# Attention values of a hybrid encoder block: three fp32r passes of split operands in place of fp32 products

## The chip, the cores and the metric

One core of a Trainium2 chip. The metric is the device time of one execution in microseconds (us). The core has five engines that run at the same time, each with a queue of its own: TensorE (PE, matrix products), VectorE (DVE), ScalarE (ACT), GpSimd (POOL) and SyncE (SP, which issues the loads here). They wait for each other by semaphores, and an engine that waits holds up everything behind the wait in its queue.

## What is computed

A block of a streaming encoder on 512 tokens of width 1024, all in fp32. Three branches (an S5 state space, a gated MLP with causal mixing, and a cross-attention into 256 memory tokens) are gated, summed, projected and added to x; a SwiGLU feed-forward with hidden width 2816 and a last RMS norm follow. What the change touches is the cross-attention, with 4 heads of width 128:

```python
kv = _rms(mem, g_mem) @ w_kv
k, v = jnp.split(kv, 2, axis=-1)
s = jnp.einsum('blhd,bmhd->bhlm', q, k) * (XA_HEAD_DIM ** -0.5)
p = jax.nn.softmax(s, axis=-1)
o = jnp.einsum('bhlm,bmhd->blhd', p, v)      # l: 512 tokens, m: 256 memory tokens
yc = o.reshape(bsz, seq, XA_WIDTH) @ w_c_out
```

## The kernel before, in words

**Split products.** Nearly all matrix products are made in three fp32r passes. An operand is kept as a high part, its value rounded to fp32r, and a low part, the value minus the high part, rounded too. `product(out, a, b, first, last)` issues high by high, high by low and low by high into one bank of PSUM (L1305 to L1307). The weights come as 512 KB tiles in a fixed order: SP loads tile t into one of two buffers (L314), ACT rounds it to `w_hi` (L460), POOL subtracts for `w_lo` (L383, or L388 in halves). Then TensorE uses the tile, and ACT may round the tile after next into the same slot. Small products stay in fp32: scores, transposes, the mixing of the gated MLP (L1477), and the products of probabilities and values (L1416).

**The attention stage**, 98 to 155 us in the trace. TensorE's order is written out by hand: `scores` of heads 0 and 1, then `value_weights(t)` (four tiles that build the values in banks 4 and 5) alternating with `zu(c)` (four tiles of the MLP's u half), with transposes and scores of later heads between them. It ends with

```python
value_weights(3)
zu(3)
pe.wait_ge(v_taken, 2)
values(0)
pe.wait_ge(exp_done, 16)
transposes(2)
values(1)
transposes(3)
```

then four mixing groups at L1477, `values(2)` and `values(3)`. The weight tiles of the gate stage (tile T_J1 and on) come next; the first gate matmul waits until DVE has added the mixing bias to all four groups (`sgu_taken`), because it uses their bank.

**One head.** `scores(h)` writes 512x256 scores. DVE finds the row maxima (`head_max`, L994 and L996), ACT takes the exponentials into `prob` (`softmax_exp`, L556), DVE multiplies by the reciprocal sums (`head_scale`, L1001 and L1004). `transposes(h)` turns `prob` into two banks, one for each half of the memory tokens (L1408, fp32). `take_pt(h)` exists twice: ACT copies the first half into `pT` (L568), DVE the second (L1011), at their own places in their queues. `values(h)` waits for both and issues one fp32 product for each half (L1416). `round_o(h)` on ACT and `low_o(h)` on DVE split the result for the output product.

**The values.** After `value_weights(3)` DVE scales banks 4 and 5 by the memory norm into `vM` (L1058), 128x512 for each of two token groups.

**The queues around it.** ACT, in order: ..., rounding of tile T_VU+7, gelu_u(2), rounding of T_J1, take_pt(1), softmax_exp(3), rounding of T_J1+1, gelu_u(3), take_pt(2), round_o(0), take_pt(3), round_o(1), four `round_yb`, round_o(2), round_o(3). DVE: ..., sine and cosine tables, scale_u(2), take_pt(1), head_max(3), `vM`, `table_sum`, scale_u(3), head_scale(3), take_pt(2), low_o(0), take_pt(3), low_o(1), the bias additions and gatings. POOL, after the low part of T_J1+1: memsets of `ca[1]` (L413) once `uc` is ready, of `st` after the transposes, of `ba` and `toep` after the mixing, then `pads_ready`, on which ACT's first `spread_b` waits, and the low parts of the further tiles.

Places in SBUF: `vM` lies right behind the keys `kT` (o_a + 12288 and o_a + 8192, 4 KB each); the buffer at o_u holds `uT` early and `ca[1]` later.

Of the kernel before, what the change touches and what calls it, by code (L numbers as in the profile page):

```python
# [16 lines left out]
P = 128  # L17
D = 1024
T = 512
M = 256  # L20
KD = D // P
WB = 512
# [3 lines left out]
HEADS = 4  # L26
# [50 lines left out]
def build(nc, xt_d, xtok_d, mem_d, mtok_d, small_d, sgu_d, w_d, out_d):  # L77
# [7 lines left out]
    with ExitStack() as ctx:  # L85
# [6 lines left out]
        def at(name, off, shape, dt=F):  # L92
            return nc.alloc_sbuf_tensor_at(name, shape, dt, offset=off)
# [33 lines left out]
        memf = at("memf", o_a, [P, KD, M])  # L127
        qT = at("qT", o_a, [P, HEADS, T])
        kT = at("kT", o_a + 8192, [P, HEADS, M])
        vM = at("vM", o_a + 12288, [P, 2, WB])  # L130
        mgf = at("mgf", o_a, [P, KD, T])

        vtok = at("vtok", o_b, [P, 4, WB])
# [41 lines left out]

        mstd = at("mstd", o_f, [P, M])
        mrstd = at("mrstd", o_f + 1024, [P, M])
        pT = at("pT", o_f, [P, 2, 2, T])
        yaf = at("yaf", o_f, [P, KB, T])
        mf = at("mf", o_f, [P, 2, T])  # L180

# [27 lines left out]
        def fv(t):  # L209
            return t.bitcast(F)  # L210
# [5 lines left out]
        def sems(names):  # L216
            return [sem(n) for n in names.split()]
# [19 lines left out]
        tok_sq, tok_std, diag_x, diag_m, wide_x, wide_m, rstd_ready, mrstd_ready = sems(  # L237
            "tok_sq tok_std diag_x diag_m wide_x wide_m rstd_ready mrstd_ready")

        za_taken, zv_taken, zq_taken, k_taken, v_taken, zu_scaled, zu_ready = sems(  # L240
            "za_taken zv_taken zq_taken k_taken v_taken zu_scaled zu_ready")
        var_ready, vstd_ready, vln_ready = sems("var_ready vstd_ready vln_ready")
        sgu_done, sgu_taken, yb_f, yb_hi_s, yb_lo_s = sems("sgu_done sgu_taken yb_f yb_hi_s yb_lo_s")
        sc_done, mx_ready, exp_done, p_ready = sems("sc_done mx_ready exp_done p_ready")
# [131 lines left out]
        def _(pool):  # L376
# [31 lines left out]
                low_weights_in_halves(t % NS, t)  # L408
            for t in range(T_J1, T_J1 + NS):
                low_weights(t % NS, t)  # L410
            pool.wait_ge(uc_ready, 16)
            for i in range(2):
                nc.gpsimd.memset(ca[1][i][:, :, :, :], 0.0)  # L413
            pool.wait_ge(pt_done, HEADS)
# [39 lines left out]
        def _(act):  # L454
            def round_weights(t, m=0, per=0):

                slot = t % NS
                act.wait_ge(raw_loaded[slot], 16 * (per // 2) * m + 16 * (t // 2))
                act.wait_ge(w_used, per * m + (t + 1 - NS))
                nc.scalar.activation(w_hi[:, slot, :], raw[:, slot, :], ACT.Copy).then_inc(w_rounded, 1)  # L460
# [88 lines left out]
            def softmax_exp(h):  # L549
                for tt in range(4):  # L550
                    act.wait_ge(mx_ready, 2 * h + tt // 2 + 1)
                    if h >= 2:
                        act.wait_ge(pt_done, h - 1)
                    i = 4 * h + tt
                    b = SCORE_BANK[h] + tt // 2
                    nc.scalar.activation(prob[:, i % 8, :], bank[b][:, (tt % 2) * M:(tt % 2 + 1) * M], ACT.Exp,  # L556
                                         bias=snm[:, i:i + 1], scale=SCALE, accum_out=ssum[:, i:i + 1]
                                         ).then_inc(exp_done, 1)
# [5 lines left out]
            def take_pt(h):  # L564
                act.wait_ge(pt_done, h + 1)
                if h >= 2:
                    act.wait_ge(pv_done, h - 1)
                nc.scalar.activation(pT[:, h % 2, 0, :], bank[PT_BANK[h]][:, :], ACT.Copy).then_inc(pt_act, 1)  # L568

            def round_o(h):  # L570
                act.wait_ge(pv_done, h + 1)
# [19 lines left out]
            round_weights(T_J1)  # L591
            take_pt(1)
            softmax_exp(3)
            round_weights(T_J1 + 1)
            gelu_u(3)
            take_pt(2)
# [200 lines left out]
        def _(dve):  # L797
# [207 lines left out]
                                    ).then_inc(p_ready, 1)  # L1005

            def take_pt(h):
                dve.wait_ge(pt_done, h + 1)
                if h >= 2:
                    dve.wait_ge(pv_done, h - 1)  # L1010
                V.tensor_copy(pT[:, h % 2, 1, :], bank[PT_BANK[h] + 1][:, :]).then_inc(pt_dve, 1)  # L1011

            def low_o(h):
                dve.wait_ge(o_hi_s, h + 1)
# [38 lines left out]
            scale_u(2)  # L1053
            take_pt(1)
            head_max(3)
            dve.wait_ge(w_used, T_VU + 7)
            for c in range(2):
                V.tensor_scalar(vM[:, c, :], bank[4 + c][:, :], mtrstd[:, c:c + 1], None, ALU.mult  # L1058
                                ).then_inc(v_taken, 1)
            table_sum(NC // 2, 1).then_inc(tables_ready, 1)  # L1060
            scale_u(3)
            head_scale(3)
# [237 lines left out]
        def _(pe):  # L1300
            mm = nc.tensor.matmul

            def product(out, a, b, first, last):

                mm(out, a[0], b[0], start=first, stop=False)  # L1305
                mm(out, a[0], b[1], start=False, stop=False)  # L1306
                return mm(out, a[1], b[0], start=False, stop=last)  # L1307
# [102 lines left out]
                ins.then_inc(pt_done, 1)  # L1410

            def values(head):
                pe.wait_ge(pt_act, head + 1)
                pe.wait_ge(pt_dve, head + 1)
                for half in range(2):
                    ins = mm(bank[4 + head % 2][:, :], vM[:, half, head * P:(head + 1) * P], pT[:, head % 2, half, :],  # L1416
                             start=half == 0, stop=half == 1)
                ins.then_inc(pv_done, 1)

            def value_weights(t):  # L1420
# [30 lines left out]
            zu(1)  # L1451
            value_weights(2)
            zu(2)
            pe.wait_ge(pt_act, 1)
            pe.wait_ge(pt_dve, 1)
            transposes(1)
            pe.wait_ge(exp_done, 12)
            scores(3)
# [11 lines left out]
            for g in range(4):  # L1470
                if g < 2:
                    pe.wait_ge(zu_scaled, 3 + g)
                else:
                    pe.wait_ge(pt_act, 3)
                    pe.wait_ge(pt_dve, 3)
                for b in range(4):
                    ins = mm(bank[SGU_BANK[g]][:, b * P:(b + 1) * P], vtok[:, b, g * P:(g + 1) * P],  # L1477
                             sgu[:, 3, g * P:(g + 1) * P], start=True, stop=True)
                ins.then_inc(sgu_done, 1)
# [4 lines left out]


            pe.wait_ge(sgu_taken, 4)
            pe.wait_ge(pt_act, 4)

            def responses(m):

# [317 lines left out]
```

## Time and profile before

| what | before |
|---|---|
| median of 3 runs | 813.68 us (812.5 to 813.94) |
| profiled execution, device time | 813.09 us |
| its span, first to last instruction | 811.4 us |
| busy: PE / DVE / ACT / POOL | 790.8 / 413.4 / 356.6 / 354.1 us |
| share of the chain that ended last on PE | 84% |
| mean granted TensorE clock | 0.986 of 2.4 GHz |

The device time of the profiled execution is 1.7 us longer than its span: that much lies around the first and last instruction. Times in the trace count from the start of the span. A TensorE record overlaps the next one: the time from start to start is what a matmul costs in a row of them, and its own length includes the flow through the array. A timeline row may merge several instructions (x4); "[1.17 <-DVE prob L1004]" says that the engine was idle for 1.17 us and that this result ended it. The granted clock is 1.00 at 2.4 GHz and 0.50 at 1.2 GHz.

### The profile page before, as it was taken

Reading aid. Unit: us, or ns where it says so; the run is one execution under the profiler, and the core shown is the slowest. Engines: PE = TensorE matmul, PEld = TensorE weight load, DVE = VectorE, ACT = ScalarE, POOL = GpSimd, SP = SyncE. Lnnn points to the kernel's source line nnn. Section 1 sums busy time; section 2 is a strip of 40 time slices with the busy share of each in tenths; the row PEclk is TensorE's granted clock in tenths of the full one; section 3 lists DMA queues with packets and bytes.
Section 4 is the critical chain, followed back from the end, with each engine's and each line's share of the span. In section 5 each row is a group of like instructions: output and inputs, shape, how many; then the busy total and the mean of one; then the engine's idle time right before and its main releaser. Section 6 shows DMA issues by size and latency. Waiting matters only on the chain.

```text
span 811.4 us, 10169 instructions
## 1 busy us (share of the span) xinstructions
PE 790.8 (97%) x3690; PEld 655.9 (81%) x3690; DVE 413.4 (51%) x625; ACT 356.6 (44%) x520; POOL 354.1 (44%) x182
## 2 busy tenths in 40 slices
PE   7999799999999999999999999999999999999996
PEld 6788687688888888888788788888888888888885
DVE  5899969856566665246765533333333333000035
ACT  5796355633535333634434444444433443122133
POOL 2556646234242434444344344444444444443452
PEclk8999899999999999999999999999999999999997
DMA  7743323022221343232323223322332233233313
GB/s 240 288 153 105 129 72 108 29 79 86 71 91 65 100 160 105 78 102 80 104 83 99 102 82 102 103 97 84 103 103 86 95 103 101 85 100 103 99 57 104
DMA packets 24814, 83.90 MB, mean 103 GB/s; under 512 B 2640, under 2 KB 4816, under 8 KB 24400
## 3 DMA queue, kind: packets, MB, share of 16 engines
q1 hardware_dynamic: 24784, 83.50, 31.0%
q8 instruction: 19, 0.31, 0.1%
q14 instruction: 11, 0.09, 0.0%
HBM read 81.39 MB, written 2.10 MB: 103 GB/s over the span
## 4 chain that ended last, share of the span: by engine, by line
PE 84%; DVE 9%; issue 3%; POOL 2%; DMA 1%; ACT 1%; SPq 0%; POOLq 0%; DVEq 0%; ACTq 0%
PE bank L1305 26%; PE bank L1307 26%; PE bank L1306 26%; DVE pow_tmp L803 2%; POOL w_lo L383 1%; PE bank L1514 1%; PE bank L1399 1%; PE bank L1524 1%; PE bank L1416 1%; DMA raw<-w_dram 1%; DVE vtok L969 1%; DVE mf L1175 1%; DVE bpow L803 1%; DVE tab_tmp L803 1%; DVE cpow L803 1%
## 5 line engine op out<-in xcount | busy, mean ns | idle before, releaser
L383 POOL TENSOR_TENSOR w_lo<-raw,w_hi 128x1024 fp32r<-128x1024 f32 x111 | 268.1, 2416 | 368.1 <-ACT w_hi L460 368.1
L460 ACT ACTIVATE w_hi<-raw 128x1024 fp32r<-128x1024 f32 x133 | 141.0, 1060 | 363.4 <-PE bank L1307 353.6
L1305 PE MATMUL bank<-h_hi,w_hi 128*128 128x512 f32 x640 | 252.6, 395 | 4.9 <-DVE h_lo L808 2.2
L1306 PE MATMUL bank<-h_lo,w_hi 128*128 128x512 f32 x640 | 250.3, 391 | 0.0
L1307 PE MATMUL bank<-h_hi,w_lo 128*128 128x512 f32 x640 | 250.2, 391 | 0.0
L1305 PEld LDWEIGHTS bank<-h_hi,w_hi 128*128 128x128 f32 x640 | 120.7, 189 | 32.7 <-issue 4.4
L1307 PEld LDWEIGHTS bank<-h_hi,w_lo 128*128 128x128 f32 x640 | 120.8, 189 | 25.4
L1306 PEld LDWEIGHTS bank<-h_lo,w_hi 128*128 128x128 f32 x640 | 120.7, 189 | 25.1 <-issue 0.5
L388 POOL TENSOR_TENSOR w_lo<-raw,w_hi 128x512 fp32r<-128x512 f32 x48 | 73.6, 1553 | 60.1 <-ACT w_hi L460 51.1
L1305 PE MATMUL bank<-act_hi,w_hi 128*128 (+2 forms) x176 | 67.0, 381 | 0.0
L1307 PE MATMUL bank<-act_hi,w_lo 128*128 (+2 forms) x176 | 66.8, 379 | 0.0
L1306 PE MATMUL bank<-act_lo,w_hi 128*128 (+2 forms) x176 | 66.8, 379 | 0.0
L803 DVE TENSOR_TENSOR xT<-bank,xT 128x256 f32<-128x256 f32 (+1 forms) x24 | 12.2, 513 | 103.0 <-PE bank L1307 102.9
L803 DVE TENSOR_TENSOR actf<-bank,rstd 128x512 f32<-128x512 f32 x22 | 15.2, 691 | 62.9 <-PE bank L1307 62.9
L803 DVE TENSOR_TENSOR silu<-bank,rstd 128x512 f32<-128x512 f32 x22 | 15.1, 691 | 54.0 <-PE bank L1307 53.7
L803 DVE TENSOR_TENSOR act_lo<-actf,act_hi 128x512 f32 x22 | 38.4, 1781 | 0.0
L1306 PEld LDWEIGHTS bank<-act_lo,w_hi 128*128 128x128 f32 x176 | 33.1, 188 | 6.4
L1305 PEld LDWEIGHTS bank<-act_hi,w_hi 128*128 128x128 f32 x176 | 33.1, 188 | 6.4
L1307 PEld LDWEIGHTS bank<-act_hi,w_lo 128*128 128x128 f32 x176 | 33.1, 188 | 6.1
L803 DVE TENSOR_TENSOR actf<-actf,silu 128x512 f32<-128x512 f32 x22 | 18.3, 834 | 26.9 <-ACT silu L748 26.5
L646 ACT ACTIVATE yaf<-bank 32x128 f32<-32x128 f32 x64 | 25.0, 390 | 4.5 <-PE bank L1499 3.8
L803 DVE TENSOR_TENSOR th<-bank,rstd 128x512 f32<-128x512 f32 x16 | 10.9, 682 | 31.2 <-PE bank L1307 31.2
(248 smaller groups left out, 1128.9 us busy)
## 6 DMA issues: line engine op xcount, KB each, us to landing
raw<-w_dram SPq DMA_DIRECT2D x133, 512.0 KB, 3.4
xT<-xt_dram SPq DMA_DIRECT2D x6, 512.0 KB, 7.7
xtok<-xtok_dram SPq DMA_DIRECT2D x4, 512.0 KB, 6.6
out_dram<-xT SPq DMA_DIRECT2D x8, 256.0 KB, 2.2
raw<-w_dram SPq DMA_DIRECT2D x4, 256.0 KB, 6.9
xT<-xt_dram SPq DMA_DIRECT2D x4, 256.0 KB, 3.9
memf<-mem_dram SPq DMA_DIRECT2D x1, 1024.0 KB, 11.1
mtok<-mtok_dram SPq DMA_DIRECT2D x1, 1024.0 KB, 8.9
```

What stands on the lines that cost most here:

```text
L383: nc.gpsimd.tensor_tensor(w_lo[:, s, :], raw[:, s, :], fv(w_hi[:, s, :]), ALU.subtract).then_inc(w_ready, 1)
L388: return nc.gpsimd.tensor_tensor(w_lo[:, s, c], raw[:, s, c], fv(w_hi[:, s, c]), ALU.subtract)
L460: nc.scalar.activation(w_hi[:, slot, :], raw[:, slot, :], ACT.Copy).then_inc(w_rounded, 1)
L646: ins = nc.scalar.activation(dst[:, :, i], bank[7][32 * i:32 * i + 32, q * NC:(q + 1) * NC], ACT.Gelu_apprx_tanh)
L803: return V.tensor_tensor(out, a, b, op)
L969: V.scalar_tensor_tensor(vtok[:, c, :], vtok[:, c, :], vrs[:, c:c + 1], sgu[:, 1, :], ALU.mult, ALU.add).then_inc(vln_ready, 1)
L1175: V.scalar_tensor_tensor(mf[:, g % 2, :], prod[:, :], 0.5, mgf[:, g, :], ALU.mult, ALU.add).then_inc(j2_m, 1)
L1305: mm(out, a[0], b[0], start=first, stop=False)
L1306: mm(out, a[0], b[1], start=False, stop=False)
L1307: return mm(out, a[1], b[0], start=False, stop=last)
L1399: ins = mm(bank[b][:, j * M:(j + 1) * M], qT[:, head, t0:t0 + P], kT[:, head, :], start=True, stop=True)
L1416: ins = mm(bank[4 + head % 2][:, :], vM[:, half, head * P:(head + 1) * P], pT[:, head % 2, half, :], start=half == 0, stop=half == 1)
```

## The change

Both operands of the products at L1416 are split. `vM` becomes `vM_hi` and `vM_lo`, `pT` becomes `pT_hi` and `pT_lo`, all fp32r. `vM_lo` takes the place of the keys, `pT_lo` that of `uT` and `ca[1]`. ACT's `take_pt` copies both halves into `pT_hi`; DVE's `take_pt` waits for each and subtracts it from the bank. A new step on ACT, `round_v`, after softmax_exp(3), scales both banks into `vM_hi`, when scores of all heads and `value_weights(3)` are done; DVE then computes bank times scale minus `vM_hi` into `vM_lo`. `values(h)` issues 6 fp32r matmuls in place of 2 fp32 ones. POOL's memsets of `ca[1]` wait for the values of all four heads.

```diff
--- before.py
+++ after.py
@@ -127,7 +127,8 @@
         memf = at("memf", o_a, [P, KD, M])
         qT = at("qT", o_a, [P, HEADS, T])
         kT = at("kT", o_a + 8192, [P, HEADS, M])
-        vM = at("vM", o_a + 12288, [P, 2, WB])
+        vM_hi = at("vM_hi", o_a + 12288, [P, 2, WB], R)
+        vM_lo = at("vM_lo", o_a + 8192, [P, 2, WB], R)
         mgf = at("mgf", o_a, [P, KD, T])
 
         vtok = at("vtok", o_b, [P, 4, WB])
@@ -175,7 +176,8 @@
 
         mstd = at("mstd", o_f, [P, M])
         mrstd = at("mrstd", o_f + 1024, [P, M])
-        pT = at("pT", o_f, [P, 2, 2, T])
+        pT_hi = at("pT_hi", o_f, [P, 2, 2, T], R)
+        pT_lo = at("pT_lo", o_u, [P, 2, 2, T], R)
         yaf = at("yaf", o_f, [P, KB, T])
         mf = at("mf", o_f, [P, 2, T])
 
@@ -237,8 +239,8 @@
         tok_sq, tok_std, diag_x, diag_m, wide_x, wide_m, rstd_ready, mrstd_ready = sems(
             "tok_sq tok_std diag_x diag_m wide_x wide_m rstd_ready mrstd_ready")
 
-        za_taken, zv_taken, zq_taken, k_taken, v_taken, zu_scaled, zu_ready = sems(
-            "za_taken zv_taken zq_taken k_taken v_taken zu_scaled zu_ready")
+        za_taken, zv_taken, zq_taken, k_taken, v_taken, v_hi_s, zu_scaled, zu_ready = sems(
+            "za_taken zv_taken zq_taken k_taken v_taken v_hi_s zu_scaled zu_ready")
         var_ready, vstd_ready, vln_ready = sems("var_ready vstd_ready vln_ready")
         sgu_done, sgu_taken, yb_f, yb_hi_s, yb_lo_s = sems("sgu_done sgu_taken yb_f yb_hi_s yb_lo_s")
         sc_done, mx_ready, exp_done, p_ready = sems("sc_done mx_ready exp_done p_ready")
@@ -408,7 +410,7 @@
                 low_weights_in_halves(t % NS, t)
             for t in range(T_J1, T_J1 + NS):
                 low_weights(t % NS, t)
-            pool.wait_ge(uc_ready, 16)
+            pool.wait_ge(pv_done, HEADS)
             for i in range(2):
                 nc.gpsimd.memset(ca[1][i][:, :, :, :], 0.0)
             pool.wait_ge(pt_done, HEADS)
@@ -565,7 +567,16 @@
                 act.wait_ge(pt_done, h + 1)
                 if h >= 2:
                     act.wait_ge(pv_done, h - 1)
-                nc.scalar.activation(pT[:, h % 2, 0, :], bank[PT_BANK[h]][:, :], ACT.Copy).then_inc(pt_act, 1)
+                for half in range(2):
+                    nc.scalar.activation(pT_hi[:, h % 2, half, :], bank[PT_BANK[h] + half][:, :], ACT.Copy
+                                         ).then_inc(pt_act, 1)
+
+            def round_v():
+                act.wait_ge(sc_done, 2 * HEADS)
+                act.wait_ge(w_used, T_VU + 7)
+                for c in range(2):
+                    nc.scalar.activation(vM_hi[:, c, :], bank[4 + c][:, :], ACT.Copy, scale=mtrstd[:, c:c + 1]
+                                         ).then_inc(v_hi_s, 1)
 
             def round_o(h):
                 act.wait_ge(pv_done, h + 1)
@@ -591,6 +602,7 @@
             round_weights(T_J1)
             take_pt(1)
             softmax_exp(3)
+            round_v()
             round_weights(T_J1 + 1)
             gelu_u(3)
             take_pt(2)
@@ -1005,10 +1017,11 @@
                                     ).then_inc(p_ready, 1)
 
             def take_pt(h):
-                dve.wait_ge(pt_done, h + 1)
-                if h >= 2:
-                    dve.wait_ge(pv_done, h - 1)
-                V.tensor_copy(pT[:, h % 2, 1, :], bank[PT_BANK[h] + 1][:, :]).then_inc(pt_dve, 1)
+                dve.wait_ge(uc_ready, 16)
+                for half in range(2):
+                    dve.wait_ge(pt_act, 2 * h + half + 1)
+                    tt(pT_lo[:, h % 2, half, :], bank[PT_BANK[h] + half][:, :], fv(pT_hi[:, h % 2, half, :]),
+                       ALU.subtract).then_inc(pt_dve, 1)
 
             def low_o(h):
                 dve.wait_ge(o_hi_s, h + 1)
@@ -1053,10 +1066,10 @@
             scale_u(2)
             take_pt(1)
             head_max(3)
-            dve.wait_ge(w_used, T_VU + 7)
             for c in range(2):
-                V.tensor_scalar(vM[:, c, :], bank[4 + c][:, :], mtrstd[:, c:c + 1], None, ALU.mult
-                                ).then_inc(v_taken, 1)
+                dve.wait_ge(v_hi_s, c + 1)
+                V.scalar_tensor_tensor(vM_lo[:, c, :], bank[4 + c][:, :], mtrstd[:, c:c + 1], fv(vM_hi[:, c, :]),
+                                       ALU.mult, ALU.subtract).then_inc(v_taken, 1)
             table_sum(NC // 2, 1).then_inc(tables_ready, 1)
             scale_u(3)
             head_scale(3)
@@ -1410,11 +1423,11 @@
                 ins.then_inc(pt_done, 1)
 
             def values(head):
-                pe.wait_ge(pt_act, head + 1)
-                pe.wait_ge(pt_dve, head + 1)
                 for half in range(2):
-                    ins = mm(bank[4 + head % 2][:, :], vM[:, half, head * P:(head + 1) * P], pT[:, head % 2, half, :],
-                             start=half == 0, stop=half == 1)
+                    pe.wait_ge(pt_dve, 2 * head + half + 1)
+                    cols = slice(head * P, (head + 1) * P)
+                    ins = product(bank[4 + head % 2][:, :], (vM_hi[:, half, cols], vM_lo[:, half, cols]),
+                                  (pT_hi[:, head % 2, half, :], pT_lo[:, head % 2, half, :]), half == 0, half == 1)
                 ins.then_inc(pv_done, 1)
 
             def value_weights(t):
@@ -1451,8 +1464,8 @@
             zu(1)
             value_weights(2)
             zu(2)
-            pe.wait_ge(pt_act, 1)
-            pe.wait_ge(pt_dve, 1)
+            pe.wait_ge(pt_act, 2)
+            pe.wait_ge(pt_dve, 2)
             transposes(1)
             pe.wait_ge(exp_done, 12)
             scores(3)
@@ -1471,8 +1484,8 @@
                 if g < 2:
                     pe.wait_ge(zu_scaled, 3 + g)
                 else:
-                    pe.wait_ge(pt_act, 3)
-                    pe.wait_ge(pt_dve, 3)
+                    pe.wait_ge(pt_act, 6)
+                    pe.wait_ge(pt_dve, 6)
                 for b in range(4):
                     ins = mm(bank[SGU_BANK[g]][:, b * P:(b + 1) * P], vtok[:, b, g * P:(g + 1) * P],
                              sgu[:, 3, g * P:(g + 1) * P], start=True, stop=True)
@@ -1484,7 +1497,7 @@
 
 
             pe.wait_ge(sgu_taken, 4)
-            pe.wait_ge(pt_act, 4)
+            pe.wait_ge(pt_act, 8)
 
             def responses(m):
```

## Rows read from the trace of the kernel before

**Rows 1.** the page's chain that ended last, by engine.

```profile
PE 84%; DVE 9%; issue 3%; POOL 2%; DMA 1%; ACT 1%; SPq 0%; POOLq 0%; DVEq 0%; ACTq 0%
```

**Rows 2.** waits of TensorE from 156 us to the end, longest first.

```profile
PE bank L1682 <- DVE spread L803: 1.4, 1, 1.4
```

**Rows 3.** TensorE's timeline: start, length (us), line, operation [idle before <-releaser].

```profile
140.23 0.39 PE L1306 MATMUL bank<-h_lo,w_hi 128*128 128x512 f32 x1
140.45 0.39 PE L1307 MATMUL bank<-h_hi,w_lo 128*128 128x512 f32 x1
140.82 1.98 PE L1416 MATMUL bank<-pT,vM 128*128 128x512 f32 x4
142.64 1.04 PE L1408 MATMUL bank<-small,prob 128*128 128x128 f32 x8
...
146.56 1.09 PE L1408 MATMUL bank<-small,prob 128*128 128x128 f32 x8 [1.17 <-DVE prob L1004]
...
154.74 0.40 PE L1306 MATMUL bank<-h_lo,w_hi 128*128 128x512 f32 x1
...
168.27 0.50 PE L1305 MATMUL bank<-yb_hi,w_hi 128*128 128x512 f32 x1
```

**Rows 4.** DVE's timeline, 121 to 154 us (`prob` first alone, then all four).

```profile
121.63 0.69 DVE L803 TENSOR_TENSOR ug<-bank,rstd 128x512 f32<-128x512 f32 x1 [3.58 <-PE bank L1307]
...
135.26 0.68 DVE L1011 COPY pT<-bank 128x512 f32<-128x512 f32 x1
...
137.37 2.09 DVE L996 TENSOR_SCALAR snm<-smx 128x2 f32<-128x2 f32 x1
...
142.62 3.11 DVE L1004 TENSOR_SCALAR prob<-prob,srec 128x256 f32<-128x256 f32 x1
142.62 3.89 DVE L1004 TENSOR_SCALAR prob<-prob,srec 128x256 f32<-128x256 f32 x4
...
149.42 1.28 DVE L803 TENSOR_TENSOR th<-bank,sgu 128x512 f32<-128x512 f32 x2
...
152.80 0.69 DVE L803 TENSOR_TENSOR th<-bank,sgu 128x512 f32<-128x512 f32 x1
```

**Rows 5.** timeline of ACT, 136 to 141 us.

```profile
136.86 0.58 ACT L568 ACTIVATE pT<-bank 128x512 f32<-128x512 f32 x1
...
138.75 0.47 ACT L556 ACTIVATE prob<-bank,snm 128x256 f32<-128x256 f32 x1
...
140.47 0.21 ACT L556 ACTIVATION_READ_ACCUMULATOR prob<-bank,snm 128x1 f32 x1
```

**Rows 6.** timeline of POOL, 137 to 165 us.

```profile
137.04 2.39 POOL L383 TENSOR_TENSOR w_lo<-raw,w_hi 128x1024 fp32r<-128x1024 f32 x1 [1.26 <-ACT w_hi L460]
142.08 2.36 POOL L383 TENSOR_TENSOR w_lo<-raw,w_hi 128x1024 fp32r<-128x1024 f32 x1 [2.65 <-ACT w_hi L460]
144.37 1.21 POOL L413 MEMSET ca<- 128x640 f32 x2
...
162.04 2.39 POOL L383 TENSOR_TENSOR w_lo<-raw,w_hi 128x1024 fp32r<-128x1024 f32 x1 [7.97 <-ACT w_hi L460]
```

**Rows 7.** ACT's copies, mean ns: from a bank; from SBUF with a scale.

```profile
L572 ACT ACTIVATE o_hiT<-bank 128x512 fp32r<-128x512 f32 x4 | 2.2, 587 | 0.0
...
L473 ACT ACTIVATE h_hi<-xT,small x16: 703/709/726, 4.9 to 438.0; 128x512 fp32r<-128x512 f32 x16
```

**Rows 8.** idle stretches; windows: busy PE, PEld, DVE, ACT, POOL, granted clock.

```profile
7.26 0.51 PE L1305 MATMUL bank<-h_hi,w_hi 128*128 128x512 f32 x1 [2.23 <-DVE h_lo L808]
...
98.22 3.75 PE L1399 MATMUL bank<-kT,qT 128*128 128x256 f32 x8 [4.74 <-DVE qT L803]
...
96.47:103.30 6.83, 5.08 (x12) 4.08 (x13) 5.55 (x14) 3.31 (x13) 0.46 (x1) 0.51 0.24 77
...
7.73:14.50 6.77, 5.97 (x15) 4.20 (x14) 1.88 (x4) 4.24 (x7) 3.17 (x3) 0.51 0.74 265
...
147.00:150.00 3.00, 3.00 (x30) 3.00 (x28) 2.58 (x5) 1.09 (x2) 0.14 (x2) 1.00 0.02 8
```

## The prediction

> **What bounds the kernel now.** I read the chain that ended last first: it runs on TensorE (PE) for 84% of the span [rows 1], so what TensorE loses or wins in a stage reaches the end, unless a later wait takes it up. From 156 us to the end its longest wait is 1.4 us [rows 2], and what it waits for there (a DVE result made from its own sums) follows its own work. So the question is when the gate stage starts after the change. Its second matmul starts at 154.74 us before; a shift there moves the end by as much.
>
> Next I read the timeline of TensorE in the attention stage [rows 3]. The eight products at L1416 are fp32, and each shows as two records: four records from 140.82 to 142.64, so about 0.43 us from start to start, sixteen in all. The fp32r matmuls before them start 0.22 to 0.23 us apart. In front of `values(0)` there is almost no wait: the last fp32r matmul starts at 140.45, the next could at 140.68, and it starts at 140.82, when `vM` is ready. One wait of 1.17 us stands at 146.56, in front of `transposes(3)`, for the scaling of the probabilities of head 3.
>
> The queues of DVE, ACT and POOL over the same stretch say who delivers what [rows 4 to 6]. DVE's scaling takes 3.89 us for four instructions, the first alone 3.11 us; it ends at 145.73, 0.15 us after POOL's subtract and two memsets (142.08 to 145.58), and the other three take 0.78 us, so four alone would take 1.04. A tiny `snm` took 2.09 us and ended at 139.46; POOL's subtract before it ended at 139.43. So DVE instructions with all data in SBUF wait for POOL's to end; the copy from a bank at 135.26 has its plain 0.68 us.
>
> **The change on TensorE.** Removed: 16 records at 0.43 us, 6.9 us. Added: 24 fp32r matmuls at 0.227 us, 5.45 us. Taken alone it saves 1.4 us.
>
> **ACT and DVE, head 0.** ACT copies both halves (one more 128x512 copy), DVE then subtracts twice (0.68 us each, 0.60 from start to start). DVE waits for ACT's copy until about 117.1 us, its queue then ends near 120.2 us; before, DVE was idle for 3.58 us until 121.63 [rows 4]. Cost nothing; without that cover it would be 2 us on DVE.
>
> **Head 1 and the values, where it costs.** Before, DVE copied its half at 135.26 us. Now it waits for ACT, which reaches its copies at 136.86 [rows 5], the second 0.5 us later. Behind that wait on DVE stand head_max(3), `vM_lo`, the table sum, scale_u(3) and the scaling of head 3. Step by step: DVE subtracts from 137.5 and 138.1; head_max(3) runs from 138.7 and its last `snm` ends at 140.35. ACT's four exponentials (1.93 us, from 138.75 to 140.68 before) are released at 139.6 and end at 141.5. Only then comes `round_v`. A plain copy from a bank took 0.587 us, one from SBUF with a scale from a tensor 0.709 [rows 7]; I take 0.66 for the two together, so they end at 142.1 and 142.7. DVE's two `vM_lo`, 0.68 us each, end at 142.8 and 143.5. `values(0)` can start at 143.55 instead of 140.82: TensorE stands idle for 2.9 us where it stood for 0.14.
>
> **What the later waits take up.** At full clock `values(0)` ends at 144.9, `transposes(2)` starts at 145.0, `values(1)` at 145.9, and `transposes(3)` could start at 147.3. It waits for the scaling. DVE's table sum starts at 143.4 and takes 1.2 us. POOL's subtract of the second gate tile is released at 143.65, since the rounding is now behind `round_v`; it waits for the table sum and runs from 144.6 to 147.0 (2.36 us long, as before). The scaling waits for it as it did before and ends at 147.9 us (+0.15, +0.78). So `transposes(3)` starts at 148.0 against 146.56. The memsets of `ca[1]` are gone from there; they come after the last values, near 155 us, and push POOL's pads, ACT's spreading and the rounding of the third gate tile by 2 to 3 us. Before, its low part was ready at 164.4 us and first used at 168.27 [rows 6, 3]: no cost while the push stays under 3.8 us plus the shift itself.
>
> Then DVE: take_pt(2) from 147.85, low_o(0) at 149.05, the subtractions of head 3 after ACT's copies from 149.7, low_o(1) at 150.9, the four bias additions from 151.5 (149.42 before). From the start of the first to the end of the fourth were 4.07 us [rows 4], which gives 155.6, and the gate matmuls wait for the fourth. A first matmul after a wait takes up to 0.4 us to the second: 156.05 against 154.74, **+1.3 us** at full clock. TensorE by itself would be at its second gate matmul 8.18 us after `transposes(3)`, less 0.72 for the cheaper values of two heads: 155.45, so 0.6 us ahead. Bounds: with the scaling not held up, the same steps give +0.7; with POOL's subtract ahead of the table sum (its margin is 0.25 us) the scaling ends 1.05 us later, +2.35.
>
> **The clock.** What 2.9 us of idling does is shown by no row at this place. Earlier in this trace TensorE lost its clock of 2.4 GHz for 1.2 GHz about idle stretches of 2.23 and 4.74 us, and it kept it after the 1.17 us at 146.56 [rows 3, 8]. The new stretch is nearer to the two that lost it. After the 4.74 us it restarted at 98.22 and had 2.4 GHz back at 103.3, 5.1 us later; the low stretch after the 2.23 us lasted 6.8 us. Half of slow time is lost. I take 3.5 us after the restart, less than both, because here work follows without a break: 1.75 us lost, of which 0.65 is the slack in front of `transposes(3)`, so +1.1 us. Bounds: nothing, and 5.1 us slow, +1.9.
>
> The Trainium skill (TensorE: Matmul & The Clock Gate, HAM oscillation) speaks against this change: waiting between bursts of matmuls throttles the array, and the next burst starts cold. By it the sum is +2.4 us; without it, +1.3.
>
> **The sum.** The profiled execution took 813.09 us (span 811.4), 0.6 below the median of 813.68. +1.3 +1.1 = +2.4 gives 815.5 for it and 816.1 for the median. 0.2% of this kernel, about what a measurement can tell from no change, is 1.6 us.
>
> **Rivals.**
> - *The clock holds.* For: about both gaps that lost it TensorE had other weak stretches, and here it works without a pause on either side. Then +1.3 us: 815.0, within 0.2%. Chance 0.30.
> - *Not slower: the scaling of head 3 comes free.* Place: DVE in front of `transposes(3)`. There 2.85 us (3.89 less 1.04) were lost to POOL's subtract and memsets, and the memsets leave that place. If POOL's subtract is over when DVE reaches the scaling at 145.2 us, the wait of 1.17 us and the 1.4 us of matmul time pay for most of the stall: +0.7 us with the clock held, 814.4. Against: the subtract itself comes later. Should the stall in front of `values(0)` stay under 1 us as well, it turns faster, 812.0 or less. Chance 0.12, of which 0.04 faster.
> - *POOL's subtract goes ahead of the table sum.* +1.05 us on top: 817.1 with the clock lost, 816.0 with it held. Chance 0.07.
> - *The passes are not cheaper*: the matmuls take 0.29 us each on the new tiles, so the 1.4 us are gone. On the path lie the twelve of heads 2 and 3, +0.8 us, less the 0.6 us in hand at the gate: 816.3. Against: the pace of the weight products, 0.22 to 0.23 us with the same shapes. Chance 0.03.
> - The forecast, stall and clock lost: 0.48.
>
> **How the numbers follow.** Slower by over 0.2% (above 815.3): the forecast case but for a short slow stretch (0.42), the last two rivals (0.09), and a part of the held clock with a somewhat longer stall (0.07): 0.58. Faster 0.04, within 0.38. The range goes from 813.8 (scaling free, clock held, less 0.6 for the spread of the runs) to 817.6 (+1.3, +1.9 and the better part of +1.05) and leaves out about 2 in 10. The forecast case's own range is 815.2 to 817.0.
>
> **What would show it.** Right: a wait of TensorE of 2.5 to 3 us in front of the first values matmul, released by DVE's `vM_lo`; `transposes(3)` starting between 147.9 and 149.5 us; the scaling's first instruction over 1 us long; a granted clock below 1 somewhere from 141 to 150 us; the second gate matmul near 157.1 us (156.05 with the clock held), and every interval after it as before. Wrong: a wait under 1 us in front of `values(0)`, the gate's second matmul before 154.7, or new waits in the first gate round, where I put none.

## The result and the profile after

| what | before | after |
|---|---|---|
| median of 15 runs each | 813.98 us (811.92 to 815.64) | 815.37 us (814.12 to 816.30) |
| ratio after to before | | 1.0020, 95% interval 1.0012 to 1.0029 |
| profiled execution, device time | 813.09 us | 814.12 us |
| its span | 811.4 us | 812.4 us |
| PE / DVE / ACT busy | 790.8 / 413.4 / 356.6 us | 788.8 / 413.9 / 359.3 us |

The change makes the kernel slower by 0.2%: 1.6 us by the ratio, with an interval of 1.0 to 2.4, and 1.4 us by the medians. The direction is that of the forecast, the size is smaller than its +2.4 us.

The first lines of the page after, and its chain that ended last, by engine. TensorE is busy for 2 us less and has a smaller share of the chain [rows 1]; DVE's share is up from 9 to 12%.

```profile
span 812.4 us, 10197 instructions
...
PE 788.8 (97%) x3698; PEld 656.6 (81%) x3698; DVE 413.9 (51%) x629; ACT 359.3 (44%) x526; POOL 353.2 (43%) x182
...
PE 78%; DVE 12%; issue 4%; DMA 2%; POOL 2%; ACT 1%; SPq 1%; POOLq 0%; DVEq 0%; ACTq 0%
```

The timeline of TensorE after (start, length in us), to be read against [rows 3]:

```profile
139.43 0.39 PE L1320 MATMUL bank<-h_hi,w_lo 128*128 128x512 f32 x1
142.45 0.80 PE L1318 MATMUL bank<-pT_hi,vM_hi 128*128 128x512 f32 x1 [2.63 <-DVE vM_lo L1071]
143.04 0.63 PE L1319 MATMUL bank<-pT_lo,vM_hi 128*128 128x512 f32 x1
143.47 0.63 PE L1320 MATMUL bank<-pT_hi,vM_lo 128*128 128x512 f32 x1
...
145.18 1.28 PE L1421 MATMUL bank<-small,prob 128*128 128x128 f32 x8
...
147.68 1.04 PE L1421 MATMUL bank<-small,prob 128*128 128x128 f32 x8
...
155.38 0.50 PE L1318 MATMUL bank<-h_hi,w_hi 128*128 128x512 f32 x1 [0.34 <-DVE th L815]
155.72 0.40 PE L1319 MATMUL bank<-h_lo,w_hi 128*128 128x512 f32 x1
```

Line numbers are up by 13 here, and the products of values now stand under those of `product` (L1318 to L1320). The attention stage ran a microsecond earlier on the clock of the trace than before, so I compare intervals in place of times. Call **D** the time from the start of the last matmul of `zu(3)` (139.43; 140.45 before) to the start of the second gate matmul (155.72; 154.74 before). D was 14.29 us and is 16.29 us. From that gate matmul to the end of the span there are 656.7 us before (811.4 less 154.74) and 656.7 after (812.4 less 155.72): nothing else has moved. The span grew by 1.0 us only, because the stage began 1.0 us earlier, for a reason that is not in the change (last section).

Within D: in front of `values(0)` TensorE is idle for 2.63 us, released by DVE's `vM_lo`. Its matmuls there start 0.43 us apart (143.04 to 143.47) in place of the 0.23 at full clock. `transposes(3)` has no wait any more, and the gate waits 0.34 us for a mixing bias. The windows of the same execution (length; busy PE, PEld, DVE, ACT, POOL; granted clock; DMA) show the fall:

```profile
141.00:145.00 4.00, 2.55 (x6) 2.04 (x7) 3.96 (x6) 3.39 (x4) 2.44 (x1) 0.66 0.05 16
145.00:150.00 5.00, 5.00 (x36) 4.52 (x35) 4.13 (x8) 2.82 (x6) 0.76 (x1) 0.93 0.29 105
```

0.66 of 4 us and 0.93 of 5 us are 2.7 and 0.7 us at 1.2 GHz, 3.4 us in all, counted where the granted clock is half.

DVE, ACT and POOL after, in order of time on each [rows 4 to 6]:

```profile
136.32 1.29 DVE L815 TENSOR_TENSOR pT_lo<-bank,pT_hi 128x512 fp32r<-128x512 f32 x2 [2.20 <-ACT pT_hi L571]
...
139.03 0.17 DVE L1008 TENSOR_SCALAR snm<-smx 128x2 f32<-128x2 f32 x1
140.99 1.41 DVE L1071 SCALAR_TENSOR_TENSOR vM_lo<-bank,mtrstd,vM_hi 128x512 fp32r<-128x512 f32 x2 [1.78 <-ACT vM_hi L578]
142.31 1.22 DVE L815 TENSOR_TENSOR sinT<-tab_tmp 128x1024 f32<-128x1024 f32 x1
...
144.25 2.45 DVE L1016 TENSOR_SCALAR prob<-prob,srec 128x256 f32<-128x256 f32 x4
147.20 1.29 DVE L815 TENSOR_TENSOR pT_lo<-bank,pT_hi 128x512 fp32r<-128x512 f32 x2 [0.50 <-ACT pT_hi L571]
...
151.26 1.28 DVE L815 TENSOR_TENSOR th<-bank,sgu 128x512 f32<-128x512 f32 x2
...
154.64 0.69 DVE L815 TENSOR_TENSOR th<-bank,sgu 128x512 f32<-128x512 f32 x1
```

```profile
135.64 1.06 ACT L571 ACTIVATE pT_hi<-bank 128x512 fp32r<-128x512 f32 x2
...
138.44 0.48 ACT L558 ACTIVATE prob<-bank,snm 128x256 f32<-128x256 f32 x1 [0.44 <-DVE snm L1008]
...
140.25 1.28 ACT L578 ACTIVATE vM_hi<-bank,mtrstd 128x512 fp32r<-128x512 f32 x2
141.40 1.08 ACT L462 ACTIVATE w_hi<-raw 128x1024 fp32r<-128x1024 f32 x1
```

```profile
142.56 3.21 POOL L385 TENSOR_TENSOR w_lo<-raw,w_hi 128x1024 fp32r<-128x1024 f32 x1 [4.35 <-ACT w_hi L462]
155.10 1.20 POOL L415 MEMSET ca<- 128x640 f32 x2 [9.34 <-PE bank L1320]
...
163.88 2.39 POOL L385 TENSOR_TENSOR w_lo<-raw,w_hi 128x1024 fp32r<-128x1024 f32 x1 [6.12 <-ACT w_hi L462]
```

DVE waits 2.20 us for ACT's copies, `head_max(3)` ends its last `snm` at 139.20, ACT's first exponential waits for DVE's maxima, and `vM_hi` starts at 140.25 behind the last one; DVE waits 1.78 us for it. POOL's subtract starts at 142.56, 0.25 us after the table sum (142.31), and takes 3.21 us in place of 2.36. It ends 2.24 us after the table sum does (145.77 against 143.53), which fits a wait for the table sum to end. The scaling at 144.25 in turn waits for it, 2.45 us for four instructions; a_early_pool below shows what it takes with the subtract held back, 1.14 us. The memsets are gone to 155.10. The low part of the third gate tile ends 10.6 us after the second gate matmul starts (163.88 + 2.39 less 155.72); before it was 9.7 us [rows 6, 3]. That is 0.9 us later against the gate, and no wait came of it.

### The profile page after: what moved, and what is told of

Its sections match the earlier page's. It is cut to its first block, busy times and chain, and to the rows that moved or that the text cites. A ratio compares the mean times of both kernels' runs of the same rounds, so it can differ in the third digit from the quotient of the medians.

```text
span 812.4 us, 10197 instructions
## 1 busy us (share of the span) xinstructions
PE 788.8 (97%) x3698; PEld 656.6 (81%) x3698; DVE 413.9 (51%) x629; ACT 359.3 (44%) x526; POOL 353.2 (43%) x182
## 4 chain that ended last, share of the span: by engine, by line
PE 78%; DVE 12%; issue 4%; DMA 2%; POOL 2%; ACT 1%; SPq 1%; POOLq 0%; DVEq 0%; ACTq 0%
PE bank L1318 25%; PE bank L1320 24%; PE bank L1319 24%; DVE tab_tmp L815 2%; DVE pow_tmp L815 1%; POOL w_lo L385 1%; DMA raw<-w_dram 1%; PE bank L1527 1%; PE bank L1537 1%; DMA xT<-xt_dram 1%; DVE vtok L981 1%; DVE cpow L815 1%; DVE mf L1188 1%; PE bank L1412 1%; DVE bpow L815 1%
## 5 line engine op out<-in xcount | busy, mean ns | idle before, releaser
L1318 PE MATMUL bank<-h_hi,w_hi 128*128 128x512 f32 x640 | 251.3, 393 | 6.1 <-POOL w_lo L390 2.8
L1320 PE MATMUL bank<-h_hi,w_lo 128*128 128x512 f32 x640 | 249.1, 389 | 0.0
L1318 PEld LDWEIGHTS bank<-h_hi,w_hi 128*128 128x128 f32 x640 | 120.1, 188 | 34.4 <-POOL w_lo L390 4.4
L1320 PEld LDWEIGHTS bank<-h_hi,w_lo 128*128 128x128 f32 x640 | 120.1, 188 | 25.3
L1318 PE MATMUL bank<-act_hi,w_hi 128*128 (+2 forms) x176 | 67.0, 381 | 0.0
L1320 PE MATMUL bank<-act_hi,w_lo 128*128 (+2 forms) x176 | 66.8, 379 | 0.0
L1320 PEld LDWEIGHTS bank<-act_hi,w_lo 128*128 128x128 f32 x176 | 33.1, 188 | 6.3
L1318 PEld LDWEIGHTS bank<-act_hi,w_hi 128*128 128x128 f32 x176 | 33.1, 188 | 6.2
```

## The experiments

All ratios are against runs of the kernel before on the same chip; D of the kernel before comes from its one profiled execution. D is read from each profile in the same way.

| kernel | D, us | clock in the stage | ratio to before (95%) |
|---|---|---|---|
| before | 14.29 | held | |
| changed | 16.29 | lost | 1.0020 (1.0012 to 1.0029) |
| changed, two more executions | 16.61, 16.58 | lost, lost | |
| changed, filler matmuls | 15.64, 15.44 | held, held | 1.0007 (0.9999 to 1.0016) |
| before, memsets late | 13.14 | held | 0.9987 (0.9978 to 0.9996) |
| before, passes alone (3 executions) | 15.24, 13.62, 13.63 | lost, held, held | 1.0000 (0.9987 to 1.0013) |
| before, memsets late and passes | 12.49 | held | 0.9965 (0.9952 to 0.9979) |
| changed, values early | 14.42 | held | 0.9997 (0.9988 to 1.0007) |
| and POOL's subtract late | 13.79 | held | 0.9989 (0.9976 to 1.0002) |
| and ACT's and DVE's orders | 12.08 | held | 0.9965 (0.9950 to 0.9980) |

### Is the clock part of the price? a_filler, a_filler2, after_again, after_third

```diff
+            pe.wait_ge(pt_dve, 4)
+            for i in range(12):
+                mm(bank[2][:, :], h_hi[:, 0, 0:P], h_hi[:, 0, :], start=True, stop=True)
             pe.wait_ge(v_taken, 2)
             values(0)
```

> The changed kernel with 12 extra fp32r matmuls on TensorE (h_hi times h_hi into bank 2, which is free there, their results are never read) in front of the wait for v_taken, so that TensorE works through most of the stall. D below is the time from the start of the last matmul of zu(3) to the start of the second gate matmul: 14.29 us before, 16.29 us after the change. Theory (stall plus a stretch at 1.2 GHz that comes from it): granted clock 1.00 from 141 to 150 us, transposes(3) again waits for DVE's scaling, D 15.2 to 15.6 us, so the time is about 1 us above the kernel before, 0.7 to 1 us less than the changed kernel in a run that lost its clock. Rival (the late operands and DVE's queue set the gate start alone, the slow stretch is absorbed): D stays at 16.1 to 16.5 us.

TensorE's timeline in a_filler, DVE's `vM_lo`, and TensorE's window:

```profile
141.35 2.88 PE L1476 MATMUL bank<-h_hi 128*128 128x512 f32 x12
144.34 0.50 PE L1318 MATMUL bank<-pT_hi,vM_hi 128*128 128x512 f32 x1
...
145.84 1.04 PE L1421 MATMUL bank<-small,prob 128*128 128x128 f32 x8
...
148.66 0.55 PE L1421 MATMUL bank<-small,prob 128*128 128x128 f32 x3 [0.40 <-DVE prob L1016]
```

```profile
142.88 1.41 DVE L1071 SCALAR_TENSOR_TENSOR vM_lo<-bank,mtrstd,vM_hi 128x512 fp32r<-128x512 f32 x2 [1.79 <-ACT vM_hi L578]
```

```profile
141.00:150.00 9.00, 8.49 (x47) 6.69 (x46) 7.17 (x13) 7.06 (x15) 3.23 (x1) 1.00 0.32 103
```

The filler fills the stall and the clock is 1.00. `values(0)` starts at 144.34, 3.22 us after the last matmul of `zu(3)` and so no earlier than in the changed kernel (3.02). The filler does not hold it up either: it starts 0.05 us after `vM_lo` ends (144.29), as in the changed kernel (142.45 after 142.40). Yet D is 15.64, just above the expected range, against 16.29: with the clock held the change costs 1.35 us over the kernel before, and the slow stretch the rest. `transposes(3)` waits again for the scaling, as it does not in the changed kernel, where TensorE is the late one.

> The kernel with filler matmuls once more. Theory (without idling the clock holds each time): clock 1.00 from zu(3) to the gate, D within 0.2 us of 15.64. Rival: D varies by over 0.5 us as it does in the changed kernel.

D 15.44, clock held again: as expected, at the edge of the 0.2 us. Here `values(0)` starts 3.02 us after `zu(3)`.

> The changed kernel once more, for a second look at the stall. Theory (a wait of 2.6 us in front of values(0) in each execution; the clock falls about it as a rule): wait 2.5 to 2.8 us, a granted clock below 1 within the stage, D 16.0 to 17.2 us. Rival (the fall in the first profile was one of several outcomes): clock held and D 15.4 to 15.7 us.

> The changed kernel, a third look. Theory (the stall of 2.6 to 2.8 us costs the clock each time; only where the slow stretch lies varies): clock below 1 in the stage, D 16.0 to 17.2 us. Rival (it falls only in some executions): clock held, D 15.4 to 15.8 us.

The first values matmul and the window behind it, in after_again; the windows of after_third below:

```profile
146.34 0.50 PE L1318 MATMUL bank<-pT_hi,vM_hi 128*128 128x512 f32 x1 [2.83 <-DVE vM_lo L1071]
```

```profile
146.30:150.00 3.70, 3.66 (x13) 3.04 (x14) 3.67 (x6) 1.97 (x3) 3.20 (x1) 0.57 0.00 0
```

```profile
141.00:145.00 4.00, 2.52 (x6) 2.04 (x7) 3.95 (x6) 3.42 (x4) 2.42 (x1) 0.69 0.03 11
145.00:150.00 5.00, 5.00 (x35) 4.48 (x35) 4.02 (x8) 2.67 (x6) 0.80 (x1) 0.91 0.31 105
```

Waits of 2.83 us (just above the expected 2.8) and 2.81 us and a lost clock in both, D 16.61 and 16.58. All three profiled executions of the changed kernel lost the clock. D depends a little on how late `values(0)` is, 3.0 or 3.2 us after `zu(3)`. At 3.02 us it is 16.29 without filler and 15.44 with it, at 3.22 us 16.61 and 15.64: the slow stretch costs 0.85 and 0.97 us. The rival that it is absorbed has fallen. The timed runs point the same way (1.0007 with filler, 1.0020 without), though their intervals overlap.

### What the memsets held up: b_memset

```diff
-            pool.wait_ge(uc_ready, 16)
+            pool.wait_ge(pv_done, HEADS)
             for i in range(2):
                 nc.gpsimd.memset(ca[1][i][:, :, :, :], 0.0)
```

> The kernel before with one line of the change: POOL's memsets of ca[1] wait for the values of all heads. Theory (they are the part of the scaling's hold-up that the change takes away): the first scaling instruction ends when POOL's subtract does, near 144.6 us on the scale of before, scaling of head 3 lasts 2.7 us in place of 3.9, transposes(3) starts 1.1 us earlier without a wait, D falls from 14.29 to 13.1 to 13.4 us, and the kernel is 0.9 to 1.1 us faster than before. Rival (DVE's bias additions or POOL's later pads take it up again): D above 14.0 us, or a new wait in the first gate round, and no difference in time.

DVE's scaling of head 3, and POOL:

```profile
145.38 2.76 DVE L1004 TENSOR_SCALAR prob<-prob,srec 128x256 f32<-128x256 f32 x4
```

```profile
144.85 2.35 POOL L383 TENSOR_TENSOR w_lo<-raw,w_hi 128x1024 fp32r<-128x1024 f32 x1 [2.66 <-ACT w_hi L460]
156.37 1.20 POOL L413 MEMSET ca<- 128x640 f32 x2 [9.16 <-PE bank L1416]
```

2.76 us in place of 3.89 [rows 4]: its first instruction takes 1.98 us and ends at 147.36, 0.16 us after POOL's subtract. TensorE's wait in front of `transposes(3)` is gone, D 13.14. The kernel is 0.13% faster, 1.1 us. So this one line of the change, taken alone, is a gain; the memsets' new place late in the stage costs nothing. It suggests that the change would have cost more without this line; no run shows that, and the changed kernel needs the line, since `pT_lo` lies in the place of `ca[1]`.

### What the passes are worth: b_passes, b_passes2, b_passes3, b_memset_passes

```diff
-        vM = at("vM", o_a + 12288, [P, 2, WB])
+        vM = at("vM", o_a + 12288, [P, 2, WB], R)
...
-                    ins = mm(bank[4 + head % 2][:, :], vM[:, half, head * P:(head + 1) * P], pT[:, head % 2, half, :],
-                             start=half == 0, stop=half == 1)
+                    v, p = vM[:, half, head * P:(head + 1) * P], pT[:, head % 2, half, :]
+                    ins = product(bank[4 + head % 2][:, :], (v, v), (p, p), half == 0, half == 1)
```

> The kernel before with only TensorE's part of the change: vM and pT are fp32r, and each product of values is three fp32r passes over them. The low parts are left out of the computation: the high parts are used in all three passes, no instruction is added on ACT or DVE. Theory (24 matmuls at 0.227 us for 16 records at 0.43): TensorE is 1.4 us less busy in the stage, but the 0.7 us won on heads 0 and 1 only lengthen the wait for the scaling of head 3 from 1.17 to 1.9 us; heads 2 and 3 win 0.7 us, of which the gate start sees 0.6 to 0.7: D 13.5 to 13.8 us, and the kernel is 0.5 to 0.7 us faster. Rival (the full saving reaches the end): D 12.9 us, 1.4 us faster. Rival (passes not cheaper on these tiles): D 14.3 us or more.

> b_passes once more (fp32r passes over the high parts alone in the kernel before, low parts left out). Its wait of 1.89 us for the scaling was followed by a slow stretch, D 15.24 us. Theory (a wait of that length costs the clock only in some executions, which is why the timed runs showed no gain and no loss): this look or the next one shows the clock held and D 13.5 to 13.8 us. Rival (it costs the clock each time): D 15.0 us or more in both.

> As b_passes2, a third look at the same kernel: D 13.5 to 13.8 us with the clock held, or 14.8 us and more with it lost.

The wait for the scaling in b_passes, with the window behind it, and the windows of b_passes2 over the same work:

```profile
149.05 1.09 PE L1408 MATMUL bank<-small,prob 128*128 128x128 f32 x8 [1.89 <-DVE prob L1004]
```

```profile
149.00:153.30 4.30, 4.25 (x25) 4.26 (x26) 3.16 (x5) 1.09 (x2) 0.14 (x2) 0.63 0.14 56
```

```profile
145.00:150.00 5.00, 4.34 (x39) 4.35 (x40) 4.58 (x10) 1.08 (x2) 0.14 (x2) 1.00 0.23 85
150.00:155.00 5.00, 5.00 (x25) 4.14 (x25) 4.79 (x9) 3.05 (x6) 1.51 (x3) 1.00 0.00 0
```

b_passes2 and b_passes3 had D at 13.62 and 13.63, as the theory had it: the passes win 0.67 us of their 1.4 at the gate, the rest lengthens the wait (1.81, 1.85 and 1.89 us) for the scaling. In b_passes the clock fell behind the same wait, and D was 15.24, outside of all that was expected. That is 0.95 us worse than before, with less work on TensorE. Over the timed runs nothing is left of the gain, where 0.5 to 0.7 us had been expected. One lost clock in three executions would leave 0.13 us of it on average ((0.67 + 0.67 - 0.95) / 3), which the interval cannot tell from none; how often the timed runs lost it is not known.

> The kernel before with b_memset (POOL's memsets of ca[1] late) and b_passes (three fp32r passes over the high parts, low parts left out of the computation) together. In b_passes the win ended in a wait of 1.89 us for the scaling, after which the clock fell. Theory (the passes are worth 1.4 us once their wait is short): the wait in front of transposes(3) is 0.5 to 0.8 us, the clock stays at 2.4 GHz, D 12.3 to 12.6 us, 1.6 to 2.0 us faster than the kernel before. Rival (passes give nothing): D 13.1 us as in b_memset, or the clock falls here too.

The wait is 0.72 us, D 12.49, the clock held, and the kernel 0.35% faster, 2.8 us (1.7 to 3.9), where 1.6 to 2.0 were expected and D says 1.8. The passes gain 0.65 us over b_memset by D. With the wait short the gain is there; this is what the change was worth with its operands for free.

### Where the values stand in the queues: a_early_v

```diff
             gelu_u(2)
+            round_v()
             round_weights(T_J1)
             take_pt(1)
             softmax_exp(3)
-            round_v()
```

(and on DVE the two `vM_lo` ahead of take_pt(1))

> The changed kernel with round_v moved ahead of the rounding of tile T_J1 on ACT, and vM_lo ahead of take_pt(1) on DVE. Theory (the stall stands in front of values(0) because vM_hi comes behind the exponentials of head 3): no wait over 0.3 us in front of values(0), a short one of 0.2 to 1 us in front of transposes(2) for the exponentials instead, clock 1.00 through the stage; the gate start then hangs on DVE's chain from the scaling of head 3 over take_pt(2), take_pt(3), low_o(1) to the bias additions: D 13.7 to 14.6 us, time within 0.4 us of the kernel before, 1 to 2 us less than the changed kernel. Rival (DVE's extra passes cost as much wherever they stand): D 15.5 us or more.

TensorE's two waits for the probabilities of head 3, longest in total, its first matmul of `values(0)`, and the scaling:

```profile
PE bank L1421 <- DVE prob L1016: 1.5, 1, 1.5
...
PE bank L1421 <- ACT prob L558: 0.6, 1, 0.6
```

```profile
143.41 0.39 PE L1318 MATMUL bank<-pT_hi,vM_hi 128*128 128x512 f32 x1
```

```profile
146.20 3.26 DVE L1016 TENSOR_SCALAR prob<-prob,srec 128x256 f32<-128x256 f32 x4
```

The same instructions, two of them moved: no wait in front of `values(0)` (143.41, 0.22 us after the last matmul of `zu(3)`), 0.6 us for the exponentials, 1.5 us for the scaling, clock held, D 14.42. It is as fast as before, 1.9 us of D less than the changed kernel. So 1.1 us of D at full clock (15.5 to 14.4) and the slow stretch come from the place of `round_v` and `vM_lo`. The rest of the extra work on ACT and DVE is not free: b_memset_passes has the same products and the same late memsets without it, and its D is 12.49, 1.9 us less. In a_early_v the cheaper products (0.65) and the late memsets (1.15) together just pay for it.

### A faster order: a_early_pool, a_best

```diff
-            for t in range(T_J1, T_J1 + NS):
-                low_weights(t % NS, t)
+            low_weights(T_J1 % NS, T_J1)
+            pool.wait_ge(p_ready, 16)
+            low_weights((T_J1 + 1) % NS, T_J1 + 1)
```

> The changed kernel with round_v and vM_lo early as in a_early_v, and POOL's subtract of tile T_J1+1 held until the probabilities of head 3 are scaled. In a_early_v the scaling took 3.26 us, 2.2 of them waiting for that subtract, and TensorE waited 1.46 us for it. Theory (after the stall is gone, the next term is this hold-up): the scaling takes 1.0 to 1.2 us, no wait over 0.3 us in front of transposes(3), D (start of the last matmul of zu(3) to start of the second gate matmul) 13.0 to 13.6 us against 14.42 in a_early_v, 0.7 to 1.2 us faster than the kernel before. Rival (ACT's gelu of head group 3 with its table load sets take_pt(2), and DVE's chain the gate): D 14.0 us or more, no difference from before.

```profile
144.73 1.14 DVE L1017 TENSOR_SCALAR prob<-prob,srec 128x256 f32<-128x256 f32 x4
147.53 1.29 DVE L816 TENSOR_TENSOR pT_lo<-bank,pT_hi 128x512 fp32r<-128x512 f32 x2 [1.66 <-ACT pT_hi L572]
```

```profile
155.25 0.50 PE L1319 MATMUL bank<-h_hi,w_hi 128*128 128x512 f32 x1 [1.47 <-DVE th L816]
```

DVE's scaling (first row) now takes 1.14 us, and `transposes(3)` has no wait. But DVE waits 1.66 us for ACT's take_pt(2), which stands behind gelu_u(3) and its table load, and TensorE (last row) waits 1.47 us at the gate for the mixing bias. D 13.79 lies between what the theory (13.0 to 13.6) and the rival (14.0) expected: the hold-up was real, but of the 1.7 us by which `transposes(3)` starts earlier against `zu(3)` (4.63 after 6.33 us) the gate sees 0.63. Two thirds went into the next wait, the one the rival named. The ratio's interval reaches 1.

```diff
             take_pt(2)
             act.wait_ge(tables_ready, 1)
             round_o(0)
             take_pt(3)
             round_o(1)
+            gelu_u(3)
...
+        MIX = (2, 3, 0, 1)
...
-            pe.wait_ge(sgu_taken, 4)
+            pe.wait_ge(sgu_taken, 2)
```

(gelu_u(3) leaves its place ahead of take_pt(2); add_mix_bias, gated, round_yb and low_yb go through the groups in the order MIX)

> a_early_pool with two more orders changed: ACT does gelu_u(3) after round_o(1) instead of before take_pt(2), and DVE adds the mixing bias to groups 2 and 3 first, since their banks are the ones that the gate matmuls take, which now wait for these two alone. Theory (TensorE is the only bound once DVE's late results are off its path): no wait in front of the gate, D 12.3 to 12.8 us, 1.5 to 2.0 us faster than the kernel before, with the full split of operands. Rival (other waits take their place: mixing results late for the output products, or a slow stretch of the clock): D above 13.3 us, or new waits in the first gate round.

All waits of TensorE in a_best from 0.6 us down, of which only the one for `prob` lies in this stage:

```profile
PE bank L1427 <- ACT prob L560: 0.6, 1, 0.6
PE bank L1324 <- POOL w_lo L386: 0.5, 2, 0.3
```

No wait at the gate, D 12.08, a little better than expected; 0.35% faster than before (0.20 to 0.50), with the operands fully split. It is faster than both kernels of the case. It equals b_memset_passes in its ratio and is 0.4 us shorter by D, though that one leaves the low parts out. So the extra work of ACT and DVE is now beside the path but for the 0.6 us that TensorE waits for the exponentials.

## Why the prediction was right in direction and too high in size

- **TensorE's work.** Right. Six matmuls of `values(0)` at full clock take 1.5 us in a_filler from first to the transposes (144.34 to 145.84), and D falls by 0.67 us with the passes alone (b_passes2, b_passes3). The prediction took 0.72 us for heads 2 and 3 and let the rest go into the wait.
- **The stall in front of `values(0)`.** Right: 3.10 us from the last matmul of `zu(3)` to the first of `values(0)` was worked out, 3.02 measured (142.45 less 139.43), 3.22 and 3.19 in the two further executions; named releaser and place are those of the trace. a_early_v shows that the place of `round_v` and `vM_lo` makes it.
- **`transposes(3)` and the scaling.** With filler, where TensorE is on time, it starts 7.54 and 7.34 us after the last matmul of `zu(3)`; 7.55 was worked out (148.0 less 140.45). POOL's subtract came behind the table sum as expected, with a margin of 0.25 us (142.56 against 142.31). So the rival in which it goes first did not happen, nor did the one with a free scaling: 2.45 us, not 1.04.
- **DVE's chain and the gate at full clock.** +1.3 us was forecast; the filler runs give 15.64 and 15.44 against 14.29, +1.35 and +1.15. The agreement is that of the whole sum; its parts were not measured one by one.
- **The clock.** It was lost in all three profiled executions, as in the likeliest case; the slow stretch lasted 3.4 us in each of them, where 3.5 us after the restart were taken. That the length came out so close is luck: the two low stretches of the kernel before had lasted 5.1 us after the restart and 6.8 us, and 3.5 was a choice below both. `transposes(3)` started 8.25, 8.58 and 8.54 us after the last matmul of `zu(3)`, against 7.34 and 7.54 with filler, so 0.9 to 1.0 us later where `values(0)` is equally late. Price: +1.1 forecast, 0.85 and 0.97 measured. The Trainium skill (TensorE: Matmul & The Clock Gate, HAM oscillation) says that a wait between bursts of matmuls makes the next burst start cold. The three profiled executions of the changed kernel agree with it. But the waits of its example are longer than these, so its words alone do not settle a wait of 2.6 to 2.8 us, and of the three waits of 1.8 to 1.9 us in the passes kernel only one was followed by a slow stretch.
- **No price on the late memsets.** Right, b_memset.
- **The sum.** +2.4 us was forecast, and D says +2.0, +2.3 and +2.3. Of the 0.4 us too much in the first execution, 0.25 are the clock's (0.85 for 1.1) and 0.15 the rest's (1.15 for 1.3). The timed runs say +1.6 by the ratio (1.0 to 2.4) and +1.4 by the medians. The median of 815.37 us lies nearer to the 815.0 of the rival in which the clock holds than to the 816.1 of the forecast: it is the traces that decide between the two, not the time. Why the timed runs lie lower than D is not settled. It may be chance: for each kernel of the table the shift of D, or its mean, lies inside the interval of the timed runs. But six of the eight kernels come out lower in the timed runs than by D, so the one D of the kernel before may be lower than its usual one. It may be that this kernel loses its clock in some executions behind its wait of 1.17 us, which one profile cannot show; that was not tried.

## What to carry to other kernels

A low part that must follow a high part on another engine ties two queues together: before such a split is put in, look at what stands ahead of the new step in the first queue and behind the wait in the second, and place the step where its input is ready, not where the old one stood. Work taken off the engine that bounds the kernel is worth only what the next wait leaves of it, and a longer wait can cost TensorE its clock, and so more than the work saved. When a stall of that kind cannot be removed, matmuls without use may be cheaper than idling: here they gave back 0.85 and 0.97 us of D.

## What I had not expected of the hardware

- The same wait may or may not cost the clock: of three executions of one kernel with waits of 1.89, 1.81 and 1.85 us in front of `transposes(3)`, one had a granted clock of 0.63 over the next 4.3 us and D 1.6 us longer, two had 1.00. Waits of 2.63, 2.83 and 2.81 us were each followed by a fall; one of 1.46 us (a_early_v) was not.
- A lost clock had the same length each time: the granted clock was 0.50 for 3.4 us in all four executions that lost it in this stage. Read from windows of half a microsecond, it began 0.2 us before TensorE restarted in the first execution of the changed kernel and 1.1 us after it in b_passes. There, with no later wait to take anything up, D grew by 1.6 us, about half of the 3.4; in the changed kernel it grew by 0.85 to 0.97, since TensorE had slack in front of `transposes(3)`.
- The place of the attention stage in the trace differs by 3.9 us between executions (last matmul of `zu(3)` at 139.29 to 143.23 us), while the rest of the kernel from the gate on takes 655.8 to 656.7 us in all of them. In the changed kernel the difference goes with the wait for `qT` in front of the first scores, longer than any in this stage, and with the slow stretch behind it. With the stage early, the granted clock from 90 to 110 us was 0.91, with it late 0.74 (both the changed kernel, the second one after_again):

```profile
90.00:110.00 20.00, 14.97 (x63) 12.21 (x62) 18.77 (x33) 7.65 (x20) 9.95 (x6) 0.91 0.20 68
```

```profile
90.00:110.00 20.00, 11.93 (x47) 9.64 (x46) 18.54 (x34) 7.38 (x19) 6.46 (x5) 0.74 0.18 61
```

  The wait itself is listed with 5.0 us in the one and 8.1 us in the other. So a single profile's span says little about a change of a microsecond; intervals inside the stage do.
